# One program from attention to the end of a hybrid layer: the state-space stage's tail moves among the attention output's first products

## The reference, cut to what matters

```python
h = rmsnorm(x, norm_mix_g)
proj = h @ w_in                      # z | xBC | dt | q | k | v | gate_a | gate_b
# branch A: state-space scan over xBC, in 4 groups of 4 heads
y, h_last = ssd_scan(xs, dt, a_head, bm, cm, h0g)
y = (y + d_skip * xs) * silu(z)                          # per group of 256 channels:
y = y * lax.rsqrt(jnp.mean(y * y, axis=-1) + EPS) * mnorm_g
branch_a = y @ w_a
# branch B: stick-breaking attention
o = sb_attention(q, k_all, v_all, past)
branch_b = o @ w_b
merged = sigmoid(gate_a) * branch_a + sigmoid(gate_b) * branch_b
x = x + merged @ w_out
x = x + (silu(hf @ w_gate) * (hf @ w_up)) @ w_down       # hf = rmsnorm(x)
x = x + sigmoid(rmsnorm(x) @ w_ple_gate) * (p @ w_ple)
return rmsnorm(x), k, v, new_conv, new_ssm               # h_last becomes new_ssm
```

## Time and profile before

| | |
|---|---|
| time, median of 3 runs | 2704.05 us (2697.49 to 2707.13) |
| the profiled execution's own time | 2699.5 us |
| its span, first to last instruction | 2697.8 us |
| PE busy | 2615.7 us, 97% of the span |
| DVE, ACT, POOL busy | 1528.2, 836.3, 345.4 us |
| mean granted TensorE clock | 0.984 of full |
| chain that ended last | PE 47% of the span, nearly all of it from 1380.78 us on |

### The profile page before, as it was taken

One profiled execution on the slowest core, in us unless ns is written; L12 is line 12 of the kernel. 1 busy time (PEld: TensorE's weight loads), 2 busy tenths in 40 slices (PEclk: granted clock), 3 DMA queues, 4 the chain that ended last, 5 costly groups with the idle time before them and its releaser, 6 DMA issues. The chain is left out here.

```text
span 2697.8 us, 47913 instructions
## 1 busy us (share of the span) xinstructions
PE 2615.7 (97%) x17088; PEld 2491.2 (92%) x17088; DVE 1528.2 (57%) x2585; ACT 836.3 (31%) x1564; POOL 345.4 (13%) x327
## 2 busy tenths in 40 slices
PE   6999999999999999999979999999999999999897
PEld 6888888888879999999979999999999999999897
DVE  4666766666675757575753443545444444444754
ACT  4443434344342425343431222211111111111513
POOL 0222322322231011111100002000000000000300
PEclk8999999999999999999979999999999999999999
DMA  5444544456524141436255433411111111111112
GB/s 137 92 109 75 120 82 100 91 82 106 84 69 71 25 103 28 101 33 101 33 197 189 162 102 126 144 40 46 40 39 47 39 46 40 39 47 39 36 41 80
DMA packets 331857, 214.35 MB, mean 79 GB/s; under 512 B 117828, under 2 KB 312216, under 8 KB 331672
## 3 DMA queue, kind: packets, MB, share of 16 engines
q1 hardware_dynamic: 331672, 211.98, 33.1%
HBM read 164.51 MB, written 47.41 MB: 79 GB/s over the span
## 5 line engine op out<-in xcount | busy, mean ns | idle before, releaser
L165 PE MATMUL bank<-operand_hi,w_hi 128*128 128x384 f32 x1584 | 533.6, 337 | 1.5 <-DVE w_lo L148 1.5
L165 PE MATMUL bank<-operand_hi,w_lo 128*128 128x384 f32 x1584 | 530.7, 335 | 0.0
L165 PE MATMUL bank<-operand_lo,w_hi 128*128 128x384 f32 x1584 | 530.5, 335 | 0.0
L139 ACT ACTIVATE w_hi<-w_raw 128x1024 fp32r<-128x1024 f32 (+1 forms) x167 | 172.6, 1034 | 779.5 <-PE bank L165 485.8
L165 PEld LDWEIGHTS bank<-operand_hi,w_hi 128*128 128x128 f32 x1584 | 298.1, 188 | 2.1 <-issue 1.8
L165 PEld LDWEIGHTS bank<-operand_lo,w_hi 128*128 128x128 f32 x1584 | 298.0, 188 | 0.3
L165 PEld LDWEIGHTS bank<-operand_hi,w_lo 128*128 128x128 f32 x1584 | 297.8, 188 | 0.0
L694 PE MATMUL acc<-operand_hi,w_hi 128*128 128x384 f32 x792 | 281.3, 355 | 5.5 <-PEq L215 5.5
L1153 POOL TENSOR_TENSOR wgt<-wgt,left 128x128 f32<-128x128 f32 (+2 forms) x224 | 209.8, 942 | 580.6 <-DVE left L1105 411.6
L165 PE MATMUL sacc<-operand_hi,w_hi 128*128 128x384 f32 x768 | 266.5, 347 | 6.1 <-DVE w_lo L148 3.3
L148 DVE TENSOR_TENSOR w_lo<-w_raw,w_hi 128x1024 fp32r<-128x1024 f32 (+1 forms) x167 | 201.6, 1208 | 119.7 <-ACT w_hi L139 118.6
(11 more groups left out here) (357 smaller groups left out, 4454.5 us busy)
## 6 DMA issues: line engine op xcount, KB each, us to landing
w_raw<-in_w_in SPq DMA_DIRECT2D x65, 512.0 KB, 8.0
k_cache<-in_cache_k SPq DMA_DIRECT2D x256, 64.0 KB, 2.5
v_cache<-in_cache_v SPq DMA_DIRECT2D x64, 256.0 KB, 4.3
w_raw<-in_w_gate SPq DMA_DIRECT2D x22, 512.0 KB, 3.7
w_raw<-in_w_up SPq DMA_DIRECT2D x22, 512.0 KB, 3.8
w_raw<-in_w_down SPq DMA_DIRECT2D x22, 512.0 KB, 3.8
s_gate_a<-gate SPq DMA_DIRECT2D x24, 192.0 KB, 2.8
s_o<-o_t SPq DMA_DIRECT2D x8, 576.0 KB, 9.1
```

Of the source, the lines that this page charges most:

```text
L139: act.activation(hi, S.raw[u0 % 2][:, 0:cols], ACT.Copy).then_inc(S.hi_done, 1)
L165: last = pe.matmul(acc[:, 0:RBN], w[:, k, :], a[:, k, rows], start=(n == 0), stop=(n == 3 * kts - 1 and more is None))
```

## The change

The two blocks become one program, so no engine meets the others behind the state-space stage, and the last group's tail is dealt out over the attention stage's first pass. For that the operands change places: o goes into `operand0` (free once the last product of `w_in` is done), y into `operand1`, the merged sum into `operand0`, the feed-forward input into `operand1`. `sq_sums`, `spare`, `first_emb` and padding are laid out anew to fit. In parts:

- PE: the hardware loop over groups becomes a Python loop, so groups 1 to 3 are written out one behind the other. `sample_sums`, `norm_sums` and `spread` of group 3 move into the first attention pass, behind its steps k = 1, 3 and 5. That pass uses three banks: steps k for blocks 0 to 2 together, then blocks 3 to 5 one by one in the same banks as DVE empties them.
- DVE: in groups 0 to 2 the gating, the last state and the sample states move from the end of the loop body to the start of the next turn. In the last group the gating goes to POOL; the rest is placed among the low parts of o. The first pass's two low parts of y come behind all six gated blocks.
- ACT: high parts of o start when the last product of `w_in` is done; squares and root of the last group stand among them.
- SP: the first four loads of o move up, behind the last group's conv tail; the last group's stores and the store of y move behind the other four loads of o; the gate tiles are loaded behind these.
- Feed-forward: DVE waits for the stores of x before its first gated block instead of behind it.

```diff
+                if last:
+                    for m in range(4):
+                        sp.dma_start(xp[:, m, 0:ROWS], S.d_o[m]).then_inc(S.o_in[m], 16)
+                for j in range(4, 8):
+                    weight(j)
+                if not last:
+                    store_states(i)
                     load_h0(i + 1)
...
-            sp.wait_ge(S.tp_drained, tpv(NG - 1, "tail"))
-            for m in range(4):
-                sp.dma_start(xp[:, m, 0:ROWS], S.d_o[m]).then_inc(S.o_in[m], 16)
-            store_y(NG - 1)
-            for s, n in ((tail_st, 96), (state_st, 32), (h0_st, 32), (gb_st, 16)):
-                sp.wait_ge(s, DMA_HEAD + NG * n)
+            def last_stores():
+                store_states(NG - 1)
+                store_y(NG - 1)
+                for s, n in ((tail_st, 96), (state_st, 32), (h0_st, 32), (gb_st, 16)):
+                    sp.wait_ge(s, DMA_HEAD + NG * n)
+            S.ssd_stores = last_stores
...
             head(0, True)
-            with pe.Fori(1, NG) as i:
+            for i in range(1, NG):
                 rest(i - 1)
                 head(i, False)
             rest(NG - 1)
-            sample_sums(NG - 1)
-            norm_sums(NG - 1)
-            spread(NG - 1)
+            S.ssd_sums = sample_sums, norm_sums, spread
+            S.ssd_free = HEAD + t0 + NTP2 * (NG - 1) + SSD_TP.index("state")
...
-            squares(NG - 1, 0)
-            squares(NG - 1, 1)
-            roots(NG - 1)
+            S.ssd_squares = squares, roots
...
-            def sample_states(i):
-                outputs(i, PT)
+            def gated(i):
                 for q in range(2):
...
+            def last_state(i):
...
+            def sample_states(i):
...
+                else:
+                    gated(i - 1)
+                    last_state(i - 1)
+                    sample_states(i - 1)
...
-                sample_states(i)
+                outputs(i, PT)
...
             body(0, True)
             with dve.Fori(1, NG) as i:
                 body(i, False)
-            norm_factors(NG - 1)
-            norm(NG - 1)
+            S.ssd_norm = last_state, sample_states, norm_factors, norm
...
+            with pool.Fori(0, NG - 1) as i:
+                silu(i)
+                squares_added(i)
+            i = NG - 1
+            silu(i)
+            for q in range(2):
+                pool.wait_ge(y_read, START + RT * i + RT)
+                pool.wait_ge(silu_z, START + 2 * i + q + 1)
+                pool.tensor_tensor(y[:, q, :], y[:, q, :], zt[:, q, :], ALU.mult).then_inc(gate_mul, 1)
+            squares_added(i)
...
-        for m in range(KT):
-            if m >= 4:
...
-                sp.wait_ge(lo_done, m - 3)
-                sp.dma_start(first_src[m % 4][:, :], S.d_o[m]).then_inc(src_in[m % 4], 16)
-            if m in (3, 4):
-                load_gate(0, m - 3)
-
-
+        for m in range(4, KT):
+            sp.wait_ge(lo_done, m - 3)
+            sp.dma_start(first_src[m % 4][:, :], S.d_o[m]).then_inc(src_in[m % 4], 16)
+        S.ssd_stores()
+        for j in range(2):
+            load_gate(0, j)
...
+        sample_sums, norm_sums, spread = S.ssd_sums
+        pe.wait_ge(S.tp_drained, S.ssd_free)
         for k in range(KT):
             pe.wait_ge(lo_done, k + 1)
-            for n in range(6):
-                hi, lo = parts[n // 3]
-                for m, (w, a) in enumerate(((hi, S.R1_hi), (hi, S.R1_lo), (lo, S.R1_hi))):
-                    last = pe.matmul(acc[n][:, 0:RBN], w[:, k, :], a[:, k, rb_cols(n % 3)],
+            hi, lo = parts[0]
+            for n in range(3):
+                for m, (w, a) in enumerate(((hi, S.R0_hi), (hi, S.R0_lo), (lo, S.R0_hi))):
+                    last = pe.matmul(acc[n][:, 0:RBN], w[:, k, :], a[:, k, rb_cols(n)],
                                      start=(k == 0 and m == 0), stop=(k == KT - 1 and m == 2))
                 if k == KT - 1:
                     last.then_inc(S.acc_done, 1)
+            if k == 1:
+                sample_sums(NG - 1)
+            if k == 3:
+                norm_sums(NG - 1)
+            if k == 5:
+                spread(NG - 1)
+        for n in range(3, 6):
+            product_block(S, pe, (u0 + 1) % 2, acc[n - 3], (S.R0_hi, S.R0_lo), n - 3,
+                          HEAD + u0 + 2, (S.acc_read_v, HEAD + bv0 + n - 2))
         with pe.Fori(1, KT // 2) as i:
             for n in range(6):
-                product_block(S, pe, (u0 + n // 3) % 2, acc[n], (S.R1_hi, S.R1_lo), n % 3,
-                              HEAD + u0 + 2 * i + n // 3 + 1, (S.acc_read_v, HEAD + bv0 + 6 * i + n - 5))
+                product_block(S, pe, (u0 + n // 3) % 2, acc[n], (S.R0_hi, S.R0_lo), n % 3,
+                              HEAD + u0 + 2 * i + n // 3 + 1, (S.acc_read_v, HEAD + bv0 + 6 * i + n - 2))
...
+        squares, roots = S.ssd_squares
+
+        def high(m):
             act.wait_ge(src_in[m % 4], 16 * (m // 4 + 1))
-            act.activation(S.R1_hi[:, m, :], first_src[m % 4][:, :], ACT.Copy).then_inc(hi_done, 1)
-        with act.Fori(0, KT // 2) as i:
+            act.activation(S.R0_hi[:, m, :], first_src[m % 4][:, :], ACT.Copy).then_inc(hi_done, 1)
+
+        act.wait_ge(S.acc_done, HEAD + b0)
+        for m in range(4):
+            high(m)
+        squares(NG - 1, 0)
+        squares(NG - 1, 1)
+        high(4)
+        high(5)
+        roots(NG - 1)
+        high(6)
+        high(7)
+
+        def pass_(i):
             for j in range(2):
                 act.wait_ge(src_in[j], 16 * (KT // 4 + 1) + 16 * i)
-                act.activation(flat_tile(S.R0_hi, 2 * i + j), src_t[j][:, :], ACT.Copy).then_inc(hi_done, 1)
...
                 S.W.split_hi(act, u0 + j + 2, 2, i, HEAD + b0 + 6 * i + 3 * j + 3)
 
+        for j in range(2):
+            S.W.split_hi(act, u0 + j + 2, 2, 0, HEAD + b0 + 3 * j + 3)
+        for j in range(2):
+            act.wait_ge(src_in[j], 16 * (KT // 4 + 1))
+            act.activation(flat_tile(S.R1_hi, j), src_t[j][:, :], ACT.Copy).then_inc(hi_done, 1)
+        with act.Fori(1, KT // 2) as i:
+            pass_(i)
+
     def vector(dve):
-        for m in range(KT):
+        last_state, sample_states, norm_factors, norm = S.ssd_norm
+
+        def low(m):
             dve.wait_ge(hi_done, m + 1)
-            if m == 3:
-                dve.wait_ge(S.y_stored, DMA_HEAD + 16 * NG)
-            dve.tensor_tensor(S.R1_lo[:, m, :], first_src[m % 4][:, :], S.R1_hi[:, m, :].bitcast(F32),
+            dve.tensor_tensor(S.R0_lo[:, m, :], first_src[m % 4][:, :], S.R0_hi[:, m, :].bitcast(F32),
                               ALU.subtract).then_inc(lo_done, 1)
-        with dve.Fori(0, KT // 2) as i:
+
+        for m in range(3):
+            low(m)
+        last_state(NG - 1)
+        sample_states(NG - 1)
+        low(3)
+        norm_factors(NG - 1)
+        for m in range(4, KT):
+            low(m)
+        norm(NG - 1)
+
+        def gated(i, n, a):
+            j = n // 3
+            if n % 3 == 0:
+                dve.wait_ge(gate_in[j], 16 * i + 16)
+                dve.wait_ge(stored[j], DMA_HEAD + 16 * i)
+            dve.wait_ge(S.acc_done, HEAD + b0 + 6 * i + n + 1)
+            dve.tensor_tensor(out[j][:, rb_cols(n % 3)], a[:, 0:RBN], gate[j][:, rb_cols(n % 3)],
+                              ALU.mult).then_inc(S.acc_read_v, 1)
+            if n % 3 == 2:
+                S.W.split_lo(dve, u0 + j + 2, 2, i, HEAD + b0 + 6 * i + 3 * j + 3)
+
+        def y_low(i, j):
+            dve.wait_ge(hi_done, 2 * i + KT + j + 1)
+            dve.tensor_tensor(flat_tile(S.R1_lo, 2 * i + j), src_t[j][:, :],
+                              flat_tile(S.R1_hi, 2 * i + j).bitcast(F32), ALU.subtract).then_inc(lo_done, 1)
+
+        for n in range(6):
+            gated(0, n, acc[n % 3])
+        y_low(0, 0)
+        y_low(0, 1)
+        with dve.Fori(1, KT // 2) as i:
             for n in range(6):
-                j = n // 3
-                if n % 3 == 0:
-                    dve.wait_ge(gate_in[j], 16 * i + 16)
-                    dve.wait_ge(stored[j], DMA_HEAD + 16 * i)
-                dve.wait_ge(S.acc_done, HEAD + b0 + 6 * i + n + 1)
-                dve.tensor_tensor(out[j][:, rb_cols(n % 3)], acc[n][:, 0:RBN], gate[j][:, rb_cols(n % 3)],
-                                  ALU.mult).then_inc(S.acc_read_v, 1)
+                gated(i, n, acc[n])
                 if n % 3 == 1:
-                    dve.wait_ge(hi_done, 2 * i + KT + j + 1)
-                    dve.tensor_tensor(flat_tile(S.R0_lo, 2 * i + j), src_t[j][:, :],
-                                      flat_tile(S.R0_hi, 2 * i + j).bitcast(F32), ALU.subtract)\
-                       .then_inc(lo_done, 1)
...
@@ -2454,9 +2528,9 @@
         dve.wait_ge(steps.sem, 3)
         steps.base = 3
         steps.body(0, F_PASS)
-        gate_up(0, "up0", 0)
         for st in S.x_stored:
             dve.wait_ge(st, DMA_HEAD + 16 * KT // 2)
+        gate_up(0, "up0", 0)
         for m in range(6):
```

(37 more changed lines are left out.)

68 lines of the change are left out of this document (24 added, 44 removed).

## The result

The changed kernel takes **2718.77 us** (median of 5 runs, 2715.48 to 2721.24) against 2704.05 before: ratio 1.0064, 95% interval 1.0052 to 1.0076, slower by 14 to 21 us. The forecast was 2700.5 with a range to 2710, "slower" at 0.10. The profiled execution of after took 2717.66, its span is 2715.9.

What follows compares the result with a forecast made beforehand. PE, busy 97% of the span, was taken as the bound, so only its stalls or half clock mattered. Terms -9.5 (loop), +5.2 (tail), +0.8 (second pass) gave -3.5; from median 2704.05 the forecast was 2700.5 us, range 2690.5 to 2710.

Steps and rivals of the forecast that it cites:

- Behind S both kernels do the same products: From the second attention pass on, PE's work was taken as unchanged; only a wait of 0.8 us was added.
- S: Start of the attention stage's second pass on PE, 1408.90 before; forecast 1414.1, 5.2 us later without the loop's gain.
- D: Time from S to the start of the last product; forecast +0.8 us.
- The loop: Writing out PE's groups removes idle gaps at two hardware-loop jumps and half clock behind them: -9.5 us.
- B: Time from the second group's first transpose of hist to the fourth's, holding both jumps; forecast -9.5 us.
- The tail: Last group's tail among first attention products: PE waits for low parts, norm and gate tile 0; +5.2 us.
- C: Time from the fourth group's first transpose of hist to S; forecast +5.2 us.
- GpSimd went first: Bounds case: POOL's gating product issues before DVE's low 0, so low 0 ends at 1362.6, PE starts 2.6 us later.
- The second pass: Blocks there need the block three before read out, not six; wait for a late gate load, 0.8 us taken.
- VectorE's jump: DVE's loop jump now falls ahead of the gating; put at nothing, without cover a fetch of 2.8 us twice.
- The late gate: Rival: gate tile 0, loaded on SP behind the stage's stores, lands after 1411; 2712 us and up; chance 0.10.
- A: Start of the state-space stage's first product, ahead of the groups; forecast change 0.

Runs made afterwards that it cites:

- The 96 bytes: Changed kernel with operand 1 placed 96 bytes higher, so both halves begin at a multiple of 128 bytes: 2704.88 us, ratio to before 1.0021.
- op1_up_128: Changed kernel with gate loads ahead of last stores, last gating on VectorE, low 3 ahead of the last state, and operand 1 128 bytes higher: 2700.09 us.
- loop_only: Kernel before with only TensorE's hardware loop over the groups written out: 2700.65 us, ratio 0.9992.
- tail_loop_kept: Changed kernel with operand 1 96 bytes higher, gate loads and low 3 earlier, last gating on VectorE, TensorE's hardware group loop back: 2701.72 us, ratio 1.0002.
- gates_early: Changed kernel with the loads of gate tiles 0 and 1 ahead of the stage's last stores: 2711.22 us, ratio to before 1.0029.
- op0_before_up_32: Kernel before with operand 0 and all that is placed behind it 32 bytes higher: 2709.24 us.
- before_again: Kernel before, unchanged, profiled once more: 2706.34 us.
- other_loops_out: Kernel before with TensorE's attention, merge and output loops written out and the loop over groups kept: 2704.32 us, ratio 1.0004.

## Why the prediction was wrong, point by point

**The step that failed** is "Behind S both kernels do the same products", on which D's price of nothing but 0.8 rests. The products are the same, the place of the operand they read is not. In before the merge, the up and gate blocks and the end read operand 0, which begins at a multiple of 128 bytes. In after they read operand 1, which begins 32 bytes past one, and 9216 bytes further than before's operand 1, because the tile spare now stands ahead of it. 288 products take 50.88 instead of 49.95, and D grows by 10 to 12 us. The 96 bytes give 11.6 us back; the five profiles with operand 1 at that offset (op1_up_128 among them, 128 bytes higher) all show 176.7, the six with the whole operand at another offset 173.3 or 173.4. That the place costs this is shown. Whether the exchange of the operands would cost it without the 9216 bytes, no run tells. The diff shows both; I read them as names.

**The loop** was right in mechanism and nearly in size: -9.5 forecast; B is 274.7 on average in twelve written-out profiles and 282.4 in four with the loop and operand 0 in its place, -7.7. That the gaps go with the loop is shown by loop_only and tail_loop_kept, which change PE's code alone. What stands in them the profile shows too: all five profiles with the loop have two transfers of an instruction queue, q8, 3 to 4 us apart, at each of the two jumps, and the twelve others have none there. This queue (packets, MB, share of 16 engines) in before around the first jump (984 to 992), then in all of before and in all of after:

```profile
q8 instruction: 2, 0.03, 1.5%
```
```profile
q8 instruction: 105, 1.72, 0.3%
```
```profile
q8 instruction: 101, 1.65, 0.2%
```

The Trainium skill's page "Runtime: NRT & Kernel Launch", section "Instruction fetch mechanics", says that a taken branch can force a fetch before execution goes on; the trace agrees, with these transfers and gaps of 2.82 and 3.26 on PE, and 4.4 to 5.4 on VectorE, but for the 11.05 of tail_loop_kept. Among the twelve B varies by 4.7 us without a longer wait: gates_early waits as after does there, but its granted clock from the second group to the fourth is 0.97 instead of 0.99.

**Ahead of the groups** I had nothing, and some 3.5 us went there. That they go with the written-out groups is seen in seventeen profiles whose values overlap; the cause is open.

**The tail** had the right chain and was too cheap: C +8 to +9 instead of +5.2. GpSimd went first (1355.78 against 1356.26), which the bounds held at 2.6: PE's first product comes 135.1 after the fourth group's start, where the forecast had 132.6 (1360.0 less 1227.4 on before's clock), 2.5 later. The Trainium skill's page "SBUF — State Buffer", section "Who interferes with whom", says that issue order decides who waits; the low part issued 0.48 behind the GpSimd product, and the chain has the next one start at 1359.54, after 3.3 instead of 1.3. Of the rest, 0.8 is half clock behind the gate: S comes 14.94 behind PE's fourth block, 14.1 in the forecast. The waits themselves were as forecast: 3.80 for low 3 (4.4), 2.96 for low 4 (2.9), 7.63 for the gate (7.8).

**The second pass** paid none of the 0.8: 1104 products in a row in 196.13.

**VectorE's jump** ahead of the gating was put at nothing. Right in after, where the hole of 5.0 is hidden, though I had called it 2.8; tail_loop_kept shows what it costs without cover.

**The rival that came true** was none of the three. The late gate, the one on the slow side, was priced from a landing after 1411; the gate landed at 1399.5 on the clock of after.

Put together from the table: +3.5 in A, -7.7 in B, some +8.7 in C and +11 in D make +15.5; measured +14 to +21.

## What to carry to other kernels

When a change moves a tensor that a bound engine streams, or has it stream another one, price that itself: compare the distance of one instruction to the next in a stage that the edit leaves alone, before and after, and vary the tensor's start by 32 to 128 bytes. Work put into a hole is worth only what its own queues let through: a load behind the last stores (9.4 us) and a copy behind another job (low 3) ate what the overlap brought, and with both moved, and the gating back on VectorE, the tail is 7 us shorter than before's. Check a gain by landmarks of all stages: the written-out loop saved 8 us in its own stage, and nearly half of that was missing again ahead of it.

## What the runs showed of the hardware

In after, products of 128x384 that read operand 1 start alternately 174 and 179 to 180 ns apart, whichever half or weight they read, instead of 173, 173, 174. The offset of 32 bytes from a multiple of 128 is not enough for it: operand 0 of op0_before_up_32 has it and runs at 173.3, and before's operand 1 has it too and is slow in some profiles and one place only, the first 132 attention products, which at full clock start every 173.3 ns in before and loop_only and every 176.7 in before_again and other_loops_out. What else has to come together is open.
